# A decoder step on one core: x in two halves, products ahead of it, and the first norm's weights in front

## The reference

```python
def rmsnorm(x, w):
    y = xf * lax.rsqrt(jnp.mean(xf * xf, axis=-1, keepdims=True) + EPS)
    return y * w

hn = rmsnorm(h, p['norm_mix'][l])
proj = hn @ p['w_in'][l]
z, xbc, dt_raw, q, k, v = jnp.split(proj, SPLIT_IDX, axis=-1)
y_ssd = ssd_branch(z, xbc, dt_raw, ...)            # conv, scan, gate, norm
y_att = moba_attention(q, k_all, v_all, ...)       # samples: 1024 cached keys in pages
h = h + concat(y_ssd, y_att) @ p['w_out'][l]
h = h + cross_attend(rmsnorm(h, p['norm_ca'][l]), mem_k, mem_v, ...)
h = h + square(relu(rmsnorm(h, p['norm_mlp'][l]) @ p['w_up'][l])) @ p['w_down'][l]
```

## Time and profile before

| | |
|---|---|
| median of 3 runs | 729.7 us (728.07 to 734.04) |
| the profiled execution | 725.94 us |
| its span, first to last instruction | 724.0 us |
| mean granted TensorE clock | 0.971 of full |
| TensorE busy | 655.9 us, 91% of the span |
| VectorE busy | 427.3 us, 59% |
| ScalarE, GpSimd busy | 123.0 us and 123.1 us, 17% each |

### The profile page before, as it was taken

One profiled execution on the slowest core, in us unless ns is written; L12 is line 12 of the kernel. 1 busy time (PEld: TensorE's weight loads), 2 busy tenths in 40 slices (PEclk: granted clock), 3 DMA queues, 4 the chain that ended last, 5 costly groups with the idle time before them and its releaser, 6 DMA issues. The chain is left out here.

```text
span 724.0 us, 13005 instructions
## 1 busy us (share of the span) xinstructions
PE 655.9 (91%) x4846; PEld 511.9 (71%) x4846; DVE 427.3 (59%) x924; ACT 123.0 (17%) x305; POOL 123.1 (17%) x208
## 2 busy tenths in 40 slices
PE   5999879979999998967999967889999999999995
PEld 3756657656676555435666754468999999999994
DVE  2565355894564687776542324448977876536543
ACT  4120011010213102352110114312111110000001
POOL 6120001000120014042201300031535443000000
PEclk9999999998999999998999999999999999999998
DMA  8778777875941149654676513353545535435311
GB/s 302 227 215 303 221 247 247 257 239 152 284 126 59 59 174 274 232 144 129 180 215 259 175 43 132 117 174 118 173 126 169 160 136 200 158 135 174 118 58 65
DMA packets 102568, 126.24 MB, mean 174 GB/s; under 512 B 6427, under 2 KB 78639, under 8 KB 102514
## 3 DMA queue, kind: packets, MB, share of 16 engines
q1 hardware_dynamic: 99618, 116.25, 49.9%
q0 software_dynamic: 2896, 9.23, 4.4%
HBM read 117.16 MB, written 8.31 MB: 173 GB/s over the span
## 5 line engine op out<-in xcount | busy, mean ns | idle before, releaser
L1111 PE MATMUL ps<-hw,wring 128*128 128x288 f32 x576 | 154.1, 426 | 6.1 <-DVE qs L1993 4.9
L1111 PEld LDWEIGHTS ps<-hw,wring 128*128 128x128 f32 x576 | 112.6, 199 | 45.6 <-issue 7.4
L2100 DVE STREAM_TRANSPOSE tmp<-big 128x1024 f32<-128x1024 f32 x32 | 37.9, 1222 | 13.2 <-DMA big<-in_cache_k 10.8
L1949 DVE COPY tmp<-ps 128x512 f32<-128x512 f32 (+6 forms) x38 | 23.8, 638 | 24.7 <-PE ps L1070 20.0
L1506 PE MATMUL ps<-hw,wring 128*128 128x144 f32 x256 | 35.8, 296 | 2.2 <-DVE hw L1953 2.2
L1070 PE MATMUL ps<-ident,tmp 128*128 128x128 f32 (+2 forms) x106 | 18.4, 312 | 20.5 <-DVE tmp L2087 6.3
L1506 PEld LDWEIGHTS ps<-hw,wring 128*128 128x128 f32 x256 | 34.0, 198 | 2.7 <-DVE hw L1953 2.7
L1506 PE MATMUL ps<-big,wring 128*128 128x144 f32 x256 | 34.0, 286 | 0.0
L1070 PEld LDWEIGHTS ps<-ident,tmp 128*128 128x128 f32 (+2 forms) x106 | 12.9, 158 | 29.2 <-DVE tmp L2087 7.1
L1111 PE MATMUL ps<-attT,wring 128*128 128x288 f32 x128 | 31.4, 407 | 1.9 <-POOL attT L998 1.9
L920 POOL TENSOR_TENSOR acc<-acc,sq 128x288 f32<-128x288 f32 (+1 forms) x35 | 28.0, 799 | 27.8 <-ACT sq L1719 25.2
(11 more groups left out here) (334 smaller groups left out, 1155.2 us busy)
## 6 DMA issues: line engine op xcount, KB each, us to landing
wring<-in_w_in SPq DMA_DIRECT2D x16, 1024.0 KB, 5.7
big<-in_cache_k SPq DMA_DIRECT2D x64, 256.0 KB, 3.0
big<-in_cache_v SPq DMA_DIRECT2D x64, 256.0 KB, 3.1
wring<-in_w_up SPq DMA_DIRECT2D x16, 1024.0 KB, 5.1
wring<-in_w_down SPq DMA_DIRECT2D x16, 1024.0 KB, 4.6
wring<-in_w_ca_kv SPq DMA_DIRECT2D x4, 1024.0 KB, 7.2
big<-in_state_ssm SPq DMA_DIRECT2D x8, 512.0 KB, 6.8
wring<-in_w_out SPq DMA_DIRECT2D x4, 1024.0 KB, 4.6
```

The source lines that it names most:

```text
L1111: last = pe.matmul(ps[:, BANK[key], 0:width], w, rhs, start=(k == 0), stop=(k == K_TILES[kind] - 1))
L1949: last = dve.tensor_copy(dst, src)
L2100: dve.transpose(KT_[:, step_ % 2].rearrange("p c (w j) -> p w c j", j=32), src[:, :, :, m, :])\
```

## The change

x is loaded as two halves of 512 channels, each with its own semaphore, and the tiles 0 to 3 wait for the first alone. Before it TensorE makes 18 products of `ones` with itself into a bank that is not in use. The weights of the first norm are loaded and transposed by themselves (`"mix"`), ahead of x; the other six vectors come behind block 0 and are transposed as an item `"vec"` behind the first weight tile. VectorE scales a tile as soon as it is copied, between its own copies. Both turns of weights name VectorE as their engine.

```diff
--- before.py
+++ after.py
@@ -44,6 +44,7 @@
 
 TURN_BANKS, FEW_BANKS, SCORES = [2, 3, 6], [2, 3], 4
 UP_BANKS = [4, 5, 7]
+WARM = 18
 
 
 VEC, at = {}, 0
@@ -137,6 +138,7 @@
         unit("K", group, k)
 
     tile("qk", 0, 0)
+    item("vec")
     item("ss", "x")
     tile("qk", 0, 1)
     item("memt", 0)
@@ -360,9 +362,9 @@
 
 
 def plan_turns():
+    turn("mix", "dve")
     for c in range(DT):
         turn(("x", c))
-    turn("vec")
     for s in SEQ:
         if s == ("kt", 0, 0, 0):
             BANKS_NOW[0] = FEW_BANKS
@@ -370,6 +372,8 @@
         if s[0] == "unit" and s[1] == "MK":
             for c in range(4):
                 turn((s[1:], c, 0)), turn((s[1:], c, 1))
+        elif s[0] == "vec":
+            turn("vec", "dve")
         elif s[0] == "qrep":
             turn(("qrep", 0)), turn(("qrep", 1))
         elif s[0] == "ss":
@@ -633,7 +637,8 @@
 
             return small[:, 24 * s + a:24 * s + b]
 
-        x_in, ident_in, vec_in, const_in = sem("x_in"), sem("ident_in"), sem("vec_in"), sem("const_in")
+        x_in = [sem(f"x_in{i}") for i in range(2)]
+        ident_in, mix_in, vec_in, const_in = sem("ident_in"), sem("mix_in"), sem("vec_in"), sem("const_in")
         mem_in, cv_in, tab_in, pages_in = sem("mem_in"), sem("cv_in"), sem("tab_in"), sem("pages_in")
         dtw_in, fnorm_in = sem("dtw_in"), sem("fnorm_in")
         bias_in = [sem(f"bias_in{i}") for i in range(2)]
@@ -811,12 +816,18 @@
                             .then_inc(kv_in[n % 2], 16)
 
             sp.dma_start(ident[:, :], I["ident"]).then_inc(ident_in, 16)
-            sp.dma_start(xin[:, 0:2, :], I["x_prompt"].rearrange("(g p) n -> p g n", p=P)).then_inc(x_in, 16)
-            sp.dma_start(xin[0:NS, 2, :], I["x_sample"]).then_inc(x_in, 16)
-            for name in ("norm_mix", "norm_ca", "norm_mem", "norm_mlp", "ssd_norm", "conv_b", "conv_w"):
+
+            for i in range(2):
+                cols = slice(512 * i, 512 * i + 512)
+                sp.dma_start(xin[:, 0:2, cols], I["x_prompt"].rearrange("(g p) n -> p g n", p=P)[:, :, cols])\
+                    .then_inc(x_in[i], 16)
+                sp.dma_start(xin[0:NS, 2, cols], I["x_sample"][:, cols]).then_inc(x_in[i], 16)
+                if i == 0:
+                    sp.dma_start(vec_rows[0:DT, :], I["norm_mix"].rearrange("(r n) -> r n", n=P)).then_inc(mix_in, 16)
+            load_block(0)
+            for name in ("norm_ca", "norm_mem", "norm_mlp", "ssd_norm", "conv_b", "conv_w"):
                 rows = I[name].rearrange("(r n) -> r n", n=P)
                 sp.dma_start(vec_rows[VEC[name]:VEC[name] + rows.shape[0], :], rows).then_inc(vec_in, 16)
-            load_block(0)
             sp.dma_start(pages[0:1, :], I["page_table"].rearrange("b w -> (b w)").unsqueeze(0)).then_inc(pages_in, 16)
             load_block(1)
             sp.dma_start(memin, I["mem_prompt"].rearrange("(g p) n -> p g n", p=P)).then_inc(mem_in, 16)
@@ -1349,16 +1360,24 @@
                     last.then_inc(turn_ps, 1)
 
 
+
+            pe.wait_ge(zeros_made, 1)
+            for _ in range(WARM):
+                pe.matmul(ps[:, 7, 0:P], ones[:, :], ones[:, :], start=True, stop=True)
             pe.wait_ge(ident_in, 16)
-            pe.wait_ge(x_in, 32)
+            pe.wait_ge(mix_in, 16)
+            transposes("mix", [(vec_rows[0:DT, :], 0)])
             for c in range(DT):
+                if c % 4 == 0:
+                    pe.wait_ge(x_in[c // 4], 32)
                 transposes(("x", c), [(xin[0:n, g, c * P:(c + 1) * P], off) for g, (off, n) in enumerate(TOKS)])
-            pe.wait_ge(vec_in, 16 * 7)
-            transposes("vec", [(vec_rows[:, :], 0)])
 
             for s in SEQ:
                 if s[0] == "tile":
                     tile(*s[1:])
+                elif s[0] == "vec":
+                    pe.wait_ge(vec_in, 16 * 6)
+                    transposes("vec", [(vec_rows[:, :], 0)])
                 elif s[0] == "tab":
                     pe.wait_ge(tab_in, 16 * 6)
                     pe.wait_ge(rbx_made, 1)
@@ -1584,8 +1603,10 @@
 
             kind = key if isinstance(key, str) else key[0]
             b = bank(key)
+            if kind == "mix":
+                return vec[:, 0:DT], ps[:, b, 0:DT]
             if kind == "vec":
-                return vec[:, :], ps[:, b, 0:VROWS]
+                return vec[:, DT:VROWS], ps[:, b, DT:VROWS]
             if kind == "x":
                 return h3[:, key[1], :], ps[:, b, 0:T]
             if kind == "tab":
@@ -1780,7 +1801,6 @@
                 if c:
                     turned(act, ("x", c - 1))
                     square("x", c - 1, h3[:, c - 1, :], T)
-            leave("vec")
             turned(act, ("x", DT - 1))
             square("x", DT - 1, h3[:, DT - 1, :], T)
             for s in SEQ:
@@ -2320,13 +2340,14 @@
                 dve.tensor_tensor(hw_sums[2], b[1], a[1], ALU.subtract)
                 dve.tensor_tensor(hw_sums[3], b[0], hw_sums[1], ALU.subtract).then_inc(hs_made, 1)
 
-            for c in range(DT):
-                leave(("x", c))
-            leave("vec")
-            turned(dve, "vec")
-            for c in range(DT):
-                turned(dve, ("x", c))
-                scale_tile(hw[:, c, :], h3[:, c, :], "norm_mix", c, hw_done)
+            leave("mix")
+            turned(dve, "mix")
+            for c in range(DT + 1):
+                if c < DT:
+                    leave(("x", c))
+                if c:
+                    turned(dve, ("x", c - 1))
+                    scale_tile(hw[:, c - 1, :], h3[:, c - 1, :], "norm_mix", c - 1, hw_done)
             for i, s in enumerate(SEQ):
                 if s[0] == "tile":
                     if s[1:] == ("cao", 3, 0):
@@ -2362,6 +2383,9 @@
                     for c in range(4):
                         leave((s[1:], c, 0)), leave((s[1:], c, 1))
                     cross_bounds(s[2])
+                elif s[0] == "vec":
+                    leave("vec")
+                    turned(dve, "vec")
                 elif s[0] == "qrep":
                     leave(("qrep", 0)), leave(("qrep", 1))
                 elif s[0] == "kt":
```

## The result

The changed kernel takes 736.24 us, the median of 11 runs (732.94 to 740.75); the kernel before beside it 727.99, also of 11 (725.96 to 734.04). The ratio is 1.0114, 95% interval 1.0086 to 1.0143: slower by 1.1%, about 8 us. The forecast was no change at 730.3, with a range up to 736.0; that was 0.6 us over the 729.7 that the kernel before had in three runs, where 8.3 were measured. Ratios here compare executions in the fast state; one of e17, of 789.70 us at a mean clock of 0.842, was not, and only the median of that row has it in.

The account below looks back on a forecast made before the run. SyncE's queue, not TensorE, was taken to pace the keys. Start 0, (b) -1.2, (c) +1.2, (d) +1.8 + 0.2, (e) -1.4 give +0.6 us: 726.5 profiled, 3.8 more for the median, 730.3; range 724.5 to 736.

Parts of the forecast that it names:

- The start: First weight tiles: second tile near 16 us, 5.8 earlier; third 4.5 earlier after a 1.28 us table load on the path.
- rival D: At the start: the products do not lift the clock or transposes drop it; start gains about 3 us, time 730.3; chance 0.06.
- The head start is swallowed by SyncE's queue: At the third and fourth units of keys: they land when they land today, so the 4.5 us gained do not last.
- Rival A: At the keys: their loads also come earlier and the head start survives, 4.5 to 5 us off, 725.5; chance 0.13.
- The term is 0: What of the shorter start reaches the kernel's end: 0 us, with 1.1 us after the longer idle covered by 2.23 slack.
- rival B: At the start: the page table lands up to 2 us later and moves all gathers one for one, 732.5; chance 0.14.
- Rival C: From the third to the fourth unit of keys: TensorE stays at 1.2 GHz, +10 us, 740; chance 0.05.
- The other exchanges are of like copies beside other work: 0, bounds -0.5 and +1.: Remaining evictions that change between ScalarE and VectorE, anywhere in the kernel: 0 us, bounds -0.5 and +1.
- (b): Norm before the cross-attention: mean moves to VectorE, ScalarE's table load is hidden, path 1.2 us shorter.
- (c): Norm before the MLP: mean moves to ScalarE, its table load comes behind it on the path, +1.2 us.
- (d): First heads' result at 328.51: copy moves to VectorE, TensorE's next transposes 1.8 us later; gated norm's table load +0.2.
- (e): In cross-attention: last head's and probabilities' copies change engine, sum -1.4 us, bounds -2.0 and +0.8.

Follow-up runs that it names:

- e17: Changed kernel plus 16 unused products filling TensorE's wait for the third unit of keys, a repeat run: 736.76 us, ratio 1.0110 to the kernel before.
- e4: Changed kernel with evicting engines put back as before, plus the page table loaded ahead of everything else: 729.99 us, ratio 1.0013 to the kernel before.
- e14: Kernel before with only the page table's load moved later, behind block 1 and the memory's load: 733.21 us, ratio 1.0067 to the kernel before.
- e5: Changed kernel with only the three dtok copies given back to ScalarE: 731.87 us, ratio 1.0051 to the kernel before.
- e6: Changed kernel with dtok's, all four ohead turns' and the MLP norm's mean on their old engines: 726.52 us, ratio 0.9983 to the kernel before.

## Why the prediction was wrong

**The start: right.** The second tile was forecast near 16 us and came at 17.37; the third's gain was forecast as 4.5 and is 3.4: GpSimd's additions began at 9.84, not at 9.0, and took 6.89 us. The table load of 1.28 us stands on the path as said. The rival D is out: the first tile ran at full clock.

**The head start is swallowed by SyncE's queue: right, and shown.** The fourth unit came 0.22 us later than before with 3.4 us of head start up to the third, and e4 and e14 move it by moving one small load of SyncE's. Rival A is out with it.

**"The term is 0": wrong by 3.6 us.** Two pieces were seen. One is the page table. The prediction gave it 0.9 us late to 0.7 early and took 0; the mean over the profiles is 1.2 late, rival B in small, and e14 confirms its price of one for one. The other is the clock behind the longer wait. The prediction saw 1.1 us of it and let the 2.23 us of slack at the fourth unit cover it. In the profile they did there, but the stretch from 60 to 110 us was granted 0.86 for 0.97, and what was lost behind the fourth unit had no slack: "SyncE waits for neither" was read from 7 to 90 us, and from 90 to 150 SyncE waits 12.3 us for TensorE, for 10.1 before, so late products made late keys. Filling the wait gave back 3 to 4 us with the engines back. Rival C asked for a low clock up to the fourth unit; it lasted 3.4 us there, so C did not happen as written, and its clock cost came later and in less. How the 3.6 us split between the two pieces is not settled.

**The failed step: "The other exchanges are of like copies beside other work: 0, bounds -0.5 and +1."** The `dtok` copies were in it, and they alone cost 4.6 us (e5). A copy of the same bank to the same buffer is alike in its own 0.2 us and not in what is queued ahead of it: ScalarE idle for 15.86 us, VectorE with 3.19 us of updates. The prediction had named this place as the one that could break it, without pricing it. Without `dtok` the exchange comes to next to nothing (e5 1.0051, engines back 1.0049), near the +0.6 forecast for all of it. That nearness is in part luck: by e6 pieces of about 5 us each way stand behind it, where the prediction had terms of 1 to 2 us.

**The clock was left out of every exchange.** The waits of terms (b), (c) and (d) are in the trace about as priced: TensorE's wait ahead of the cross-attention is 3.66 us for 4.89; the MLP's load waits 1.24 for 0.22; the wait behind `ohT` is 1.86 where there was none (13 transposes ran through from 328.51). (e) was mis-sized: 1.4 us are won at 458.54 and the last head's 1.37 us vanish as said, but 0.7 are lost at 472.60 and a new wait of 1.38 follows, because ScalarE's `ohT` copy stands ahead of an exponential. With one more of 0.37 the waits sum to -0.3 us, and the stage loses 2.4 us for -1.4 forecast; the clock was down from 472.7 to 479.5, and before not in this stage. From 400 to 520 us the granted clock was 0.94 for 0.96, from 200 to 300 us 0.91 for 0.97: the sum had terms for waits and none for this. The page "TensorE: Matmul & The Clock Gate" of the Trainium skill, section "HAM oscillation — how this bites in real kernels", describes such a pattern, a wait for data with work at the lower clock behind it. The traces agree for the waits ahead of the third unit of keys (3.40 us, and 5.81 for 4.15 behind it); at 267.25 the wait was of 1.50 us and for a bank, not for data.

## What to carry to other kernels

Where a rule of thumb deals out work to two engines (here, by turns), an edit that adds or names one entry re-deals everything behind it; name the engines of the entries that matter, and price each copy by what is queued ahead of it on its new engine. A head start that ends at a queue is worth nothing unless the first thing that queue waits for goes out earlier too; e14's late small load cost 4.9 us. Read for the whole way to the end whether that queue waits for the engine, not only up to the place where the head start is lost. And a new wait of TensorE amid dense work can cost more than its length (here 1.50 us, and 5.8 in its stage against e5): read the granted clock of the stretch behind it before calling it small.

## What the runs showed that was not expected

Behind TensorE's wait of 1.50 us, which ended at 267.25, the clock was at 1.2 GHz from 267.9 on. But a wait isn't needed: before, it fell at 272.2 with no wait of more than 0.28 us in the 10 us ahead. And 4.41 us of transposes behind the first products left it at 2.4 GHz (the tile behind them took 4.15 us). The table load costs its 1.28 us and nothing more: at 508.58 it begins and at 509.88 the root does. Executions of one kernel differed by up to 10 us (723.19 to 733.08 in e4) with mean clocks that differed too, so a single profile says where time is lost, not how much.
